# A decoder trunk on one core: another written-out order of steps for the second layer's attention

## The reference, cut to what matters

```python
D_MODEL, SEQ, DEPTH, MEM_LEN, HEAD_DIM, D_FF = 1024, 512, 2, 256, 64, 2816
# layer 0: stick-breaking attention (12 heads) and 4 memory heads, then a ConvFFN
k_flat, v_flat = jnp.split(rmsnorm(h, kv_norm) @ w_kv_shared, 2, axis=-1)
# layer 1
proj = rmsnorm(x, norm_attn) @ w_in
q_dil, q_mem = jnp.split(proj, [DIL_WIDTH], axis=-1)
for g, (window, dilation) in enumerate(((128, 1), (512, 4), (2048, 16))):   # 4 heads each
    hs = slice(g * HEADS_PER_GROUP, (g + 1) * HEADS_PER_GROUP)
    o_g, lse_g = dilated_window_attention(q_dil[:, :, hs], k_sh[:, :, hs], v_sh[:, :, hs], slopes[hs], window, dilation)
alpha = jax.nn.softmax(jnp.stack(lses, axis=0), axis=0)
o_dil = jnp.concatenate([o * alpha[g][..., None].astype(o.dtype) for g, o in enumerate(outs)], axis=2)
o_mem = memory_branch(q_mem, mem, norm_mem, w_mem_kv)
x = x + jnp.concatenate([o_dil.reshape(b, s_len, DIL_WIDTH), o_mem], axis=-1) @ w_out
return x + conv_ffn(rmsnorm(x, norm_ffn), ffn_up, ffn_conv, ffn_down)
```

## Time and profile before

| | us |
|---|---|
| median of 3 runs | 1259.37 (1257.91 to 1260.78) |
| profiled execution, its time | 1259.37 |
| its span, first to last instruction | 1257.6 |
| TensorE busy in the span | 1213.7 |
| VectorE busy | 809.1 |
| ScalarE busy | 556.0 |
| mean granted TensorE clock | 0.997 |

### The profile page before, as it was taken

How to read it: one execution, slowest core, us unless ns; L and a number is a source line. 1 busy time by engine, 2 the same in 40 slices (tenths; PEclk the granted TensorE clock), 3 DMA queues, 4 the chain that set the end, 5 groups by cost and what they waited for, 6 DMA issues and landing times.

```text
span 1257.6 us, 16992 instructions
## 1 busy us (share of the span) xinstructions
PE 1213.7 (97%) x5975; PEld 997.6 (79%) x5975; DVE 809.1 (64%) x1251; ACT 556.0 (44%) x918; POOL 100.9 (8%) x133
## 2 busy tenths in 40 slices
PE   4899999999999999999999999999999999999998
PEld 3777887787788888878887878778788888878886
DVE  4866666667777777752247776877777777774226
ACT  5545665554444444441235553534544444442222
POOL 0300333333000000000002000001100000000000
PEclk9999999999999999999999999999999999999999
DMA  7421211212333333322250122122233333333552
GB/s 228 127 67 51 65 52 36 67 49 69 89 96 100 100 100 91 94 99 101 89 162 27 58 67 83 53 68 67 84 101 100 100 93 91 100 112 96 130 142 72
DMA packets 175701, 112.51 MB, mean 89 GB/s; under 512 B 20062, under 2 KB 167838, under 8 KB 175646
## 3 DMA queue, kind: packets, MB, share of 16 engines
q1 hardware_dynamic: 175646, 111.79, 29.9%
HBM read 107.58 MB, written 2.10 MB: 87 GB/s over the span
## 4 chain that ended last, share of the span: by engine, by line
PE 78%; DVE 10%; issue 5%; ACT 4%; POOL 2%; DMA 1%; DVEq 0%; SPq 0%; POOLq 0%; ACTq 0%
PE bank L1361 16%; PE bank L1362 16%; PE bank L1363 16%; PE bank L1648 8%; PE bank L1675 8%; DVE w_lo L893 2%; PE bank L1661 2%; DVE y_lo L899 2%; PE bank L1688 2%; ACT w_hi L584 1%; PE bank L1455 1%; POOL ar L564 1%; PE bank L1476 1%; PE bank L1788 1%; POOL ar L542 1%
## 5 line engine op out<-in xcount | busy, mean ns | idle before, releaser
L1361 PE MATMUL bank<-y_hi,w_hi 128*128 128x512 f32 x928 | 366.8, 395 | 8.4 <-DVEq L1033 3.9
L1363 PE MATMUL bank<-y_hi,w_lo 128*128 128x512 f32 x928 | 361.9, 390 | 0.0
L1362 PE MATMUL bank<-y_lo,w_hi 128*128 128x512 f32 x928 | 361.7, 390 | 0.0
L893 DVE TENSOR_TENSOR w_lo<-raw,w_hi 128x1024 fp32r<-128x1024 f32 x188 | 232.3, 1235 | 157.7 <-ACT w_hi L584 154.2
L584 ACT ACTIVATE w_hi<-raw 128x1024 fp32r<-128x1024 f32 x186 | 196.3, 1055 | 278.4 <-PE bank L1363 133.6
L1361 PEld LDWEIGHTS bank<-y_hi,w_hi 128*128 128x128 f32 x928 | 174.5, 188 | 49.4 <-issue 9.7
L1363 PEld LDWEIGHTS bank<-y_hi,w_lo 128*128 128x128 f32 x928 | 174.4, 188 | 36.8
L1362 PEld LDWEIGHTS bank<-y_lo,w_hi 128*128 128x128 f32 x928 | 174.6, 188 | 36.1 <-issue 1.2
L1648 PE MATMUL bank<-ar,w_hi 128*128 (+1 forms) x288 | 88.8, 389 | 0.8 <-DVE af L1125 0.8
L753 ACT ACTIVATE af<-af,conv 128x512 f32<-128x512 f32 x88 | 63.0, 716 | 35.8 <-DVE af L1125 35.8
L1675 PE MATMUL bank<-w_hi,ar 128*128 128x512 f32 x288 | 77.1, 389 | 0.8 <-DVE af L1125 0.8
(11 more groups left out here) (200 smaller groups left out, 1619.2 us busy)
## 6 DMA issues: line engine op xcount, KB each, us to landing
raw<-in_a_ffn_up SPq DMA_DIRECT2D x44, 512.0 KB, 3.8
raw<-in_b_ffn_up SPq DMA_DIRECT2D x44, 512.0 KB, 3.8
raw<-in_a_ffn_down SPq DMA_DIRECT2D x22, 512.0 KB, 3.2
raw<-in_b_ffn_down SPq DMA_DIRECT2D x22, 512.0 KB, 3.7
raw<-in_a_w_in SPq DMA_DIRECT2D x20, 512.0 KB, 3.8
raw<-in_w_kv_shared SPq DMA_DIRECT2D x12, 512.0 KB, 3.8
raw<-in_a_w_out SPq DMA_DIRECT2D x8, 512.0 KB, 3.5
raw<-in_b_w_in SPq DMA_DIRECT2D x8, 512.0 KB, 3.8
```

Of the source, the lines that this page charges most:

```text
L893: nc.vector.tensor_tensor(w_lo[:, m % SPLIT, :], raw[:, m % RAW, :], w_hi[:, m % SPLIT, :].bitcast(F32), ALU.subtract).then_inc(lo_done, 1)
L1361: mm(bank, w[0], y[0][:, k, :], start=(k == 0), stop=False)
L1362: mm(bank, w[0], y[1][:, k, :], start=False, stop=False)
L1363: last = mm(bank, w[1], y[0][:, k, :], start=False, stop=(k == KT - 1))
```

## The change

Only the list `SEQ_B` is another one: the same 278 steps (P steps counted by k), each once, in another order and with the P steps cut in other places. The first eight output rows of O steps are drawn from a list `early` by `outs(n)`, and the second half's steps are written by a loop. The core of the diff (left out: the head of the list with the memory slots, and the lines removed behind ("T", 1, 1)):

```diff
-                 ("P", 2, 1, 0, 8), ("P", 2, 2, 0, 5), ("S", 2), ("P", 2, 2, 5, 8), ("P", 3, 0, 0, 7), ("V", 2),
-                 ("P", 3, 0, 7, 8), ("P", 3, 1, 0, 3), ("G", 0), ("P", 3, 1, 3, 8), ("R", 0), ("P", 3, 2, 0, 1),
-                 ("W", 0, 0), ("P", 3, 2, 1, 2), ("W", 0, 1), ("W", 0, 2), ("P", 3, 2, 2, 3), ("T", 0, 0),
-                 ("W", 0, 3), ("T", 0, 1), ("P", 3, 2, 3, 6), ("A", 0, 0), ("T", 0, 2), ("P", 3, 2, 6, 8),
-                 ("P", 4, 0, 0, 1), ("A", 0, 1), ("T", 0, 3), ("P", 4, 0, 1, 5), ("A", 0, 2), ("A", 0, 3), ("S", 3),
-                 ("W", 0, 4), ("P", 4, 0, 5, 7), ("W", 0, 5), ("P", 4, 0, 7, 8), ("P", 4, 1, 0, 1), ("V", 3),
-                 ("P", 4, 1, 1, 2), ("T", 0, 4), ("P", 4, 1, 2, 6), ("W", 0, 6), ("T", 0, 5), ("W", 0, 7),
-                 ("P", 4, 1, 6, 7), ("A", 0, 4), ("P", 4, 1, 7, 8), ("P", 5, 0, 0, 3), ("T", 0, 6),
-                 ("P", 5, 0, 3, 4), ("A", 0, 5), ("T", 0, 7), ("P", 5, 0, 4, 8), ("P", 5, 1, 0, 1), ("A", 0, 6),
-                 ("P", 5, 1, 1, 2), ("S", 4), ("P", 5, 1, 2, 8), ("P", 4, 2, 0, 4), ("A", 0, 7), ("S", 5),
-                 ("P", 4, 2, 4, 8), ("P", 5, 2, 0, 5), ("V", 4), ("P", 5, 2, 5, 7), ("G", 1), ("P", 5, 2, 7, 8),
-                 ("O", 0, 0), ("O", 0, 2), ("O", 0, 4), ("O", 0, 6), ("R", 1), ("O", 1, 0), ("W", 1, 0), ("W", 1, 1),
-                 ("O", 1, 2), ("O", 1, 4), ("O", 1, 6), ("T", 1, 0), ("W", 1, 2), ("W", 1, 3), ("T", 1, 1),
...
+                 ("S", 1), ("V", 1), ("P", 2, 0, 4, 8), ("P", 2, 1, 0, 8), ("P", 2, 2, 0, 5),
+                 ("S", 2), ("P", 2, 2, 5, 8), ("P", 3, 0, 0, 4), ("V", 2), ("P", 3, 0, 4, 8),
+                 ("G", 0), ("P", 3, 1, 0, 8), ("R", 0), ("W", 0, 0), ("W", 0, 1), ("P", 3, 2, 0, 3),
+                 ("T", 0, 0), ("T", 0, 1), ("W", 0, 2), ("W", 0, 3), ("P", 3, 2, 3, 6),
+                 ("A", 0, 0), ("T", 0, 2), ("P", 3, 2, 6, 8), ("A", 0, 1), ("T", 0, 3), ("P", 4, 0, 0, 3),
+                 ("A", 0, 2), ("P", 4, 0, 3, 5), ("A", 0, 3), ("W", 0, 4), ("W", 0, 5),
+                 ("S", 3), ("P", 4, 0, 5, 8), ("V", 3), ("P", 4, 1, 0, 5),
+                 ("T", 0, 4), ("T", 0, 5), ("W", 0, 6), ("W", 0, 7), ("P", 4, 1, 5, 8), ("P", 5, 0, 0, 1),
+                 ("A", 0, 4), ("T", 0, 6), ("P", 5, 0, 1, 4), ("A", 0, 5), ("T", 0, 7), ("P", 5, 0, 4, 8),
+                 ("A", 0, 6), ("S", 4), ("P", 5, 1, 0, 3), ("A", 0, 7), ("P", 5, 1, 3, 8), ("P", 4, 2, 0, 5),
+                 ("S", 5), ("P", 4, 2, 5, 8), ("P", 5, 2, 0, 3), ("V", 4), ("P", 5, 2, 3, 7),
+                 ("G", 1), ("P", 5, 2, 7, 8)] + outs(5) + [("R", 1), ("W", 1, 0), ("W", 1, 1)] + outs(3)
+        SEQ_B += [("T", 1, 0), ("T", 1, 1), ("W", 1, 2), ("W", 1, 3)] + outs(3)
+        for b in range(8):
+            SEQ_B += [("A", 1, b)] + ([("T", 1, b + 2)] if b < 6 else []) + ([("W", 1, b + 4)] if b < 4 else []) + \
+                ([("V", 5)] if b == 2 else []) + outs(3 if b < 7 else 0)
```

More of the change, by code:

```diff
@@ L310, in build, with outs @@
         OUT_KS_B = [[0, 2, 4, 6], [7, 1, 3, 5]]
-        SEQ_B = [("P", 0, 0, 0, 6), ("M", 0), ("P", 0, 0, 6, 8), ("P", 0, 1, 0, 5), ("M", 1), ("P", 0, 1, 5, 8),
[27 rows of a table removed]
+        early = [("O", q, k) for q in range(KT) for k in OUT_KS_B[0]]
+        def outs(count):
+            return [early.pop(0) for _ in range(count)]
+        SEQ_B = [("P", 0, 0, 0, 5),
[17 rows of a table added]
+                 ("G", 1), ("P", 5, 2, 7, 8)] + outs(5) + [("R", 1), ("W", 1, 0), ("W", 1, 1)] + outs(3)
[3 more added lines that the diff above has]
+                ([("V", 5)] if b == 2 else []) + outs(3 if b < 7 else 0)
+        SEQ_B += [("O", q, k) for q in (KT, KT + 1) for k in (7, 1, 3)] + [("O", KT, 5), ("O", KT + 1, 5)]
+        SEQ_B += [("O", q, k) for q in range(KT + 2, 2 * KT) for k in OUT_KS_B[1]]
         def nb(jj, s):
```

## The result

| | before | after |
|---|---|---|
| median | 1258.88 (1257.82 to 1260.78, 6 executions) | 1266.53 (1264.83 to 1268.31, 6 executions) |
| ratio, 95% interval | | 1.0059 (1.0046 to 1.0074), so +7.4 us |
| profiled execution, its time and span | 1259.37, 1257.6 | 1265.73, 1263.9 (a seventh execution) |
| stage, first P to the ConvFFN's first P | 201.06 | 207.71 |

The forecast was 1262.4, with a range of 1259.2 to 1265.2. The direction was right, the size was not, and the time lies outside the range. Of the 6.4 us between the profiled executions all lies in the changed stage, which is 6.65 us longer: it runs from 686.60 to 887.66 before, from 686.28 to 893.99 after.

What follows compares the result with a forecast made beforehand. TensorE, busy 97% of the span, was taken as the bound. Waits saved -3.4, new waits +6.4, head +0.3, fewer interruptions -0.5 (partly counted already) gave +3.0 us, so 1262.4 us, range 1259.2 to 1265.2.

Steps and rivals of the forecast that it cites:

- A(0,5): Matmul step behind A(0,4): waits 1.7 us for line 1287, starts at 805.9, +2.4 us against before at this point.
- the main term: W(0,4), W(0,5) ahead of S(3): eight scalings, 1.57 us, delay S(3)'s maxima and exponentials and line 893; paid in full.
- R(1)'s 0.24 ... goes: Second half: R(1) has 18 matmuls ahead instead of 15, coefficients take 3.7 us, so its wait of 0.24 us is saved.
- From there each batch has 9 matmuls, A and T, ... no wait, no gain: Second half: each batch gives TensorE 3.25 us against some 3.0 us of VectorE, so nothing is lost or gained.
- R(0)'s 0.24: Head: G(0) comes 9 positions earlier and R(0) stays, so its wait of 0.24 us is saved.
- The -0.5 for fewer interruptions: Whole list: TensorE changes between P or O and something else 70 times instead of 76, three interruptions fewer: -0.5 us.
- The clock was a rival: Waits at 797 to 806 let TensorE's clock fall to half, costing 1.45 us: 1263.9 us; chance 0.08.
- T(0,1)'s 0.25: Head: T(0,1) needs only its own W but waits 0.25 us more for the fourth scale.
- the +0.3 of the head: Part of the list before S(3), memory slots to A(0,3): about +0.3 us in sum.
- Rival (1): From S(5) on, the lateness is given back by waits the kernel had; +0.6 to +1.0 us remains, 1260.2 us; chance 0.20.
- the slip: Lateness of VectorE's and TensorE's chain behind S(3), counted as +2.4 us at A(0,5).
- VectorE does not bound the second half: Rival claimed it does: eight batches at 3.5 us of VectorE instead of 3.0, 2.0 us more, 1264.4 us; chance 0.12.

Runs made afterwards that it cites:

- w_first: Kernel before, with only W(0,4) and W(0,5) moved ahead of S(3): ratio 1.0012, +1.5 us; stage +1.35 us.
- f1_w_behind: Kernel after, with W(0,4) and W(0,5) put back behind S(3): ratio 1.0055, +6.9 us over before; stage +5.25 us.
- a7_ahead: Kernel before, with only A(0,7) moved 21 matmuls forward, ahead of the end of tile (5,1): ratio 1.0018, +2.3 us; stage +3.11 us.
- o_ahead: Kernel before, with only O(1,0) moved ahead of R(1): ratio 1.0014, +1.8 us; stage +2.40 us.
- f3_r_ahead: Kernel after, with R(1) and the two W behind it put back ahead of O(1,0): ratio 1.0037, +4.7 us over before; stage +5.75 us.
- f4_last_a: Kernel after, with 12 matmuls in place of 9 between A(1,6) and A(1,7): ratio 1.0044, +5.5 us over before; stage +5.94 us.
- p1_head: Kernel before, with the new order only up to A(0,3): ratio 1.0004, +0.5 us; stage +0.84 us.
- p3_second: Kernel before, with the new order only from O(0,0) on, behind the last projection matmul: ratio 1.0021, +2.6 us; stage +3.75 us.
- p2_middle: Kernel before, with the new order only from behind A(0,3) to the last projection matmul: ratio 1.0036, +4.5 us; stage +3.78 us.
- f2_a_ahead: Kernel after, with A(0,4) back at position 333, ahead of the end of tile (4,1): ratio 1.0066, +8.3 us over before; stage +10.55 us.
- w_early: Kernel before, with W(0,4) and W(0,5) moved ahead of A(0,2): ratio 0.9995, -0.6 us; stage +0.05 us.
- repaired: Kernel after, with W(0,4), W(0,5) ahead of A(0,2) and A(0,4), A(0,7), V(4), R(1), last O steps moved: ratio 1.0018, +2.3 us over before.

## Why the prediction was wrong, and where it was right

**The method held for the chain it followed.** Forecast and measured waits: T(0,4) 0 and 0; P(5,0) 1.15 and 1.02; A(0,4) 1.0 and 0.84; T(0,6) 0.6 and 0.45; A(0,5) 1.7 and 1.68; S(5) 0.8 and 1.10; V(4) 0.55 and 0.45; T(1,2) 0.4 and 0.30. A(0,5) was to start at 805.9 and did at 806.24. w_first and f1_w_behind show that the order of the scalings and S(3) costs 1.35 to 1.4 us, as the main term had it. The strict order of the queues, for which the prediction named the Trainium skill, page "TensorE: Matmul & The Clock Gate", section "Architectural detail: the array is 16× 32×32, not 1× 128×128", is what a7_ahead's rows show: 893 could have started at 818.24, when 584 had ended, and did so at 819.08, behind 986, which stood ahead of it.

**The first step that failed is "R(1)'s 0.24 ... goes".** It looked at R(1), with 18 matmuls ahead of it, and not at the step that was moved past it. O(1,0) begins a new sum in the bank that tile (5,2) still holds, and VectorE empties that bank with 1002 (before: 999) only behind the coefficients of G(1), since its queue has them first. Rows of VectorE of the kernel after:

```profile
834.88 0.37 DVE L1248 COPY st<-bank 128x8 f32<-128x8 f32 x2 [1.67 <-PE bank L1757]
...
837.91 0.69 DVE L1264 COPY st<-st 32x8 f32<-32x8 f32 x4
838.63 1.05 DVE L1002 TENSOR_TENSOR sq<-bank,rT 128x512 f32<-128x512 f32 x1
```

1002 ends at 839.68 and O(1,0) starts at 839.78. The profile lists this wait as "issue" and names no releaser, and in the trace of before it lists none there. But O(1,0) was bound by the same line before. VectorE and TensorE of the kernel before:

```profile
834.59 1.07 DVE L999 TENSOR_TENSOR sq<-bank,rT 128x512 f32<-128x512 f32 x1
...
834.61 1.06 PE L1763 MATMUL bank<-st,cs 128*128 128x8 f32 x8 [0.24 <-DVE st L1261]
835.76 0.47 PE L1544 MATMUL bank<-ar,w_hi 128*128 128x512 f32 x1
```

999 ends at 835.66 and O(1,0) starts at 835.76, again 0.10 later. O(1,0) starts 6.45 us after G(1) before, 6.42 in the kernel after and in o_ahead, 6.44 in f3_r_ahead, whatever the order. Before, R(1)'s eight small matmuls were done inside this time; in the kernel after they stand behind it, 0.81 us from R(1)'s start to that of the next step. So the term is not the listed waits (+1.37 less 0.24) but R(1)'s block: from G(1) to O(1,2), the step behind both, are 7.22 us before and 7.21 in f3_r_ahead, 8.00 in the kernel after and in o_ahead. That is +0.8 where the sum had -0.24. o_ahead and f3_r_ahead measure 0.7 and 0.9 in the stage.

**The second is "From there each batch has 9 matmuls, A and T, ... no wait, no gain".** Between A(1,6) and A(1,7) 12 matmuls stood before and 9 do after. `pt_buffer` gives batch 7 of the second half the buffer of batch 6, so ScalarE may copy T(1,7) only when A(1,6) has read it, and 1283, the residual's 1304 and 1290 follow one another on VectorE:

```profile
868.23 0.69 DVE L1283 TENSOR_TENSOR ar<-bank,ar 128x512 fp32r<-128x512 f32 x1 [2.62 <-ACT ar L849]
868.84 0.68 DVE L1304 TENSOR_TENSOR hT<-hT,bank 128x512 f32<-128x512 f32 x1
869.55 0.68 DVE L1290 TENSOR_TENSOR ar<-bank,ar 64x512 fp32r<-64x512 f32 x1
```

I took the rhythm of the loop's middle for its last turn. The wait is 0.74 us, and f4_last_a takes back 0.71. For the other seven batches the step was right: no wait of more than 0.3 us is listed.

**Terms of the wrong size.** Counted from the stage's first P, A(0,5) starts 3.0 us later than before (119.96 against 116.94), where the forecast had 2.4. Of the 0.6, the head has 0.4: in p1_head A(0,5) starts 0.74 later, and 0.3 was priced. T(0,0) waits 0.76, which is 0.5 more than before, and R(0)'s 0.24 went as forecast; the rest lies in no listed wait. From A(0,5) to G(1) the kernel loses another 1.35 (G(1) at 147.08 against 142.71), where the forecast had 0.7: S(5) waits 1.10, not 0.8, and a7_ahead gives 1.46 for A(0,7)'s place alone. The -0.5 for fewer interruptions did not appear. Listed waits grew by 5.4, from 3.3 to 8.7, and the stage by 6.65, so there is 1.2 more where the sum had a gain. f1_w_behind shows such a surplus at one place (1.40 for a wait of 1.02), f4_last_a does not (0.71 for 0.74). The starts tell most of the difference. P(5,0) stands between 512-column matmuls. Without the wait it starts 0.23 us after the one before; with it, 1.41 after, and the next one 0.34 later: that is 1.18 and 0.1 for a listed 1.02, since a matmul's record runs on past the start that the next one could have had. A(1,7) is another kind of matmul and starts 0.45 after an O matmul even without a wait (f4_last_a), 1.14 with it: 0.69. What is left of the 1.2 stays open.

**The clock was a rival with 0.08. It probably came, though not in the profiled execution of the kernel after.** Of its seven executions four have a mean clock of 0.997 and take 1264.8 to 1265.7; the other three, at 0.996 and 0.994, take 1267.4 to 1268.3, 2.4 more on average. That is the size of one or two falls, but whether and where in these three the clock fell no profile shows: this part is argued from p3_second, o_ahead, p2_middle and f2_a_ahead, which have the same waits and falls behind them. Against it speaks w_first, whose slower executions have a profile with the fall outside the stage. The price of a fall was put at 1.45; by the windows it is 1.7. My ground for the low chance was that the 1.41 us before T(0,4) left the clock alone. That was one place in one execution. The Trainium skill, page "TensorE: Matmul & The Clock Gate", section "Part 1: The HAM clock gate (the "warmup" mystery)", says that the throttled clock is the default and that activity releases it. The traces agree so far as the granted clock is 0.50 behind waits (836 to 838 in p3_second) and 1.00 again a few us later. How little idle time is enough is for the runs to say: the wait of 1.37 us at O(1,0) was followed by a fall in p3_second's profiled execution and not in that of after.

**The account.** Forecast +3.0. Up to A(0,5) +0.6, from there to G(1) +0.65. From G(1) to the ConvFFN the forecast had -0.1, and the kernel lost 2.3: 0.8 by R(1) behind O(1,0), 0.7 at A(1,7), 0.3 at T(1,2), which was forecast, and 0.4 in no listed wait. Against the forecast that is +2.4, and +6.65 in all, the stage of the profiled execution. The slower three of seven executions take 2.4 more, 1.0 on average, which makes +7.7 against +7.4 measured.

**Sums that do not come out as written.** R(0)'s 0.24 and T(0,1)'s 0.25 are in the +0.3 of the head and again in the lists of waits; they cancel. Rival (1) had +0.6 to +1.0 left of the +2.4: 2.4 less 0.6, 0.17 and 0.24 is +1.4, or +0.9 with the interruptions. Half a microsecond in two waits is 1.0 either way, not 1.2.

**Of the other rivals,** the slip was not given back: behind G(1) the kernel after nowhere gains on the one before by more than 0.1 us. VectorE does not bound the second half either: it is busy 149.4 us of 207.7, before 149.7 of 201.1. The range was too narrow because it took in errors of the waits that I had named, and no room for waits that I had not.

## What to carry to other kernels

When a step changes places with another in a written-out order, ask of both which bank, buffer and semaphore they need, and price the first and the last turn of a loop on their own. A wait that the profile doesn't list can stand behind a step that fills it: R(1) was free as long as it was done while O(1,0) waited for its bank. So take the cost of an exchange from the starts of a step ahead of both and a step behind both, and not from the listed waits. In a kernel whose TensorE is 97% busy, move a wait only if the chain behind it gets shorter: w_early took 0.86 us off one wait and found them at the next. A wait of 1 us or more that is brought into dense matmuls can have a second price, here up to 1.7 us in part of the profiled executions; a single profile may show none of it.

## What the runs showed of the hardware that I had not expected

- Waits of 1.10 to 1.89 us in dense work were followed by a fall of TensorE's granted clock to 0.50 (1.10 and 1.36 in f2_a_ahead, 1.37 in p3_second, 1.38 in o_ahead, 1.89 in a7_ahead), and so was the pair of 1.02 and 0.84 with three matmuls between (p2_middle; the same pair, within 0.02, in f3_r_ahead). The same waits left it at 1.00 in other profiles (1.10, 1.37 and the pair in after, 1.86 in w_first). Behind 2.16 and 3.50 us it fell in the one profile of each.
- Waits that all 14 profiles have say the same, so the length of a wait alone does not decide. Behind the 1.35 or 1.36 us ahead of the stage's first P the clock never fell, behind one of 1.78 or 1.79 us at 226 it fell in 2 of 14 (w_first, repaired), behind the 2.67 us of the earlier trace rows in 12 of 14 (not in a7_ahead and w_early). Windows of w_first:

```profile
226.00:228.00 2.00, 1.56 (x6) 1.46 (x7) 1.84 (x3) 0.81 (x2) 0.69 (x2) 0.84 0.00 0
228.00:230.00 2.00, 2.00 (x7) 1.72 (x7) 1.37 (x3) 1.47 (x4) 0.00 (x0) 0.50 0.18 40
```

- But for the one behind 3.50 us, each fall took 1.7 us by its windows, whatever the place (p2_middle, p3_second, o_ahead, a7_ahead, f3_r_ahead, repaired, and the two later ones of f2_a_ahead). o_ahead's two groups of executions lie 1.8 apart.
- What a fall costs depends on what follows. Counted by the starts of the same steps it is 1.6 us in p3_second, where TensorE was full behind it (O(1,0) to T(1,2): 9.47 us, in the kernel after 7.90), and nothing in p2_middle and f3_r_ahead, where A(0,5) waited for VectorE in any case.
